# Decoder step: the first modulation matrix in four column items, inputs normalized by halves, query tiles in two halves

## The reference

```python
    mod = (jax.nn.silu(c) @ w_ada + b_ada)[:, None, :]
    sh1, sc1, gt1, sh2, sc2, gt2 = jnp.split(mod, 6, axis=-1)

    h = rmsnorm(x, g_mix) * (1 + sc1) + sh1
    qa, ka, va, fa, qb, kb, vb, rb, alr, ga, gb = split_cols(h @ w_in, IN_SIZES)
    ...
```

## Time and profile before

| | |
|---|---|
| time, median of 3 runs | 1292.62 us (1291.99 to 1293.03) |
| the profiled execution | 1289.96 us, of which the span of the profile is 1288.3 us |
| busy share of the span | PE 90%, VectorE 25%, ScalarE 14%, GpSimd 4% |
| bytes moved by DMA | 500.5 MB, 388 GB/s in the mean |

### The profile page before, as it was taken

The page is one execution under the profiler, slowest core; times in us unless marked ns, Lnnn a source line. Parts: engine busy times, 40 slices in busy tenths (PEclk is TensorE's granted clock), DMA queues, the critical chain, the costliest instruction groups (busy, mean ns, idle before and its releaser), DMA issues.

```text
span 1288.3 us, 15668 instructions
## 1 busy us (share of the span) xinstructions
PE 1153.6 (90%) x5948; PEld 567.6 (44%) x5948; DVE 324.2 (25%) x592; ACT 174.1 (14%) x344; POOL 48.2 (4%) x95
## 2 busy tenths in 40 slices
PE   5999999999999998889897979797988889797987
PEld 2788756687543442424242424333232424242433
DVE  2379965433122021011101110201111011101133
ACT  2132232100211100200020011002000200020102
POOL 1121122000000000000000000000000000000000
PEclk9999999999998999999999999999999999999998
DMA  9998999975979999999999999999999999999994
GB/s 349 352 375 284 378 330 394 398 317 192 411 318 416 412 418 416 420 415 421 414 423 414 422 414 421 415 419 417 418 419 416 419 415 422 414 421 411 417 417 180
DMA packets 109310, 500.52 MB, mean 388 GB/s; under 512 B 11721, under 2 KB 13879, under 8 KB 73808
## 3 DMA queue, kind: packets, MB, share of 16 engines
q1 hardware_dynamic: 102416, 478.39, 92.4%
q0 software_dynamic: 6576, 21.42, 4.6%
q10 hardware_dynamic: 272, 0.09, 0.0%
HBM read 496.48 MB, written 3.38 MB: 388 GB/s over the span
## 4 chain that ended last, share of the span: by engine, by line
PE 61%; DMA 21%; SPq 13%; issue 2%; ACT 2%; DVE 1%; DVEq 0%
PE ps L983 20%; DMA ring<-in_w_d 17%; SPq L2296 12%; PE ps L474 11%; PE ps L1043 8%; PE ps L1145 4%; PE ps L936 3%; PE ps L800 2%; PE ps L853 2%; DMA ring<-in_w_ada 2%; DMA ring<-in_w_gu 2%; PE ps L408 2%; PE ps L885 1%; PE ps L439 1%; PE ps L648 1%
## 5 line engine op out<-in xcount | busy, mean ns | idle before, releaser
L983 PE MATMUL ps<-ring,zone 128*64 128x512 f32 x2000 | 439.1, 594 | 22.4 <-DMA ring<-in_w_gu 22.4
L1043 PE MATMUL ps<-ring,oT 128*64 128x512 f32 x1024 | 232.7, 600 | 71.0 <-DMA ring<-in_w_d 70.3
L983 PEld LDWEIGHTS ps<-ring,zone 128*64 128x64 f32 x2000 | 139.8, 137 | 318.0 <-issue 277.5
L1043 PEld LDWEIGHTS ps<-ring,oT 128*64 128x64 f32 x1024 | 69.6, 137 | 231.8 <-issue 123.1
L1996 DVE TENSOR_SCALAR zone<-ps 128x1024 f32<-128x1024 f32 x15 | 18.4, 1225 | 587.2 <-PE ps L983 587.2
L474 PE MATMUL ps<-hT,ring 128*128 128x264 f32 x640 | 148.1, 389 | 2.1 <-DVE hT L1573 1.8
L474 PEld LDWEIGHTS ps<-hT,ring 128*128 128x128 f32 x640 | 119.8, 190 | 29.1 <-issue 7.7
L1412 ACT ACTIVATE attn<-zone 128x1024 f32<-128x1024 f32 x15 | 15.9, 1057 | 457.1 <-DVE zone L1996 457.1
L2013 DVE TENSOR_TENSOR zone<-zone,ps 128x264 f32<-128x264 f32 x56 | 24.1, 430 | 140.0 <-PE ps L1145 140.0
L408 PE MATMUL ps<-ident,zone 128*128 128x128 f32 (+3 forms) x212 | 32.3, 277 | 16.2 <-DMA zone<-in_b_alpha 10.6
L936 PE MATMUL ps<-zone,tok 128*128 128x224 f32 x224 | 44.2, 356 | 0.0
(11 more groups left out here) (389 smaller groups left out, 766.8 us busy)
## 6 DMA issues: line engine op xcount, KB each, us to landing
ring<-in_w_gu SPq DMA_DIRECT2D x250, 1024.0 KB, 19.8
ring<-in_w_d SPq DMA_DIRECT2D x124, 1024.0 KB, 18.4
ring<-in_w_ada SPq DMA_DIRECT2D x12, 2048.0 KB, 11.9
ring<-in_w_in SPq DMA_DIRECT2D x9, 2048.0 KB, 13.4
ring<-in_cache_k SPq DMA_DIRECT2D x32, 256.0 KB, 7.5
ring<-in_cache_k POOLq DMA_DIRECT2D x32, 256.0 KB, 6.5
ring<-in_cache_v SPq DMA_DIRECT2D x32, 256.0 KB, 9.7
ring<-in_cache_v POOLq DMA_DIRECT2D x32, 256.0 KB, 8.2
```

What stands on the lines that cost most here:

```text
L983: ins = pe.matmul(ps[64 * j:64 * j + CAP, c, :], xg[:, k, 2 * par + j, :], rows, start=False, stop=(k == KT - 1), skip_group_check=True)
L1043: ins = pe.matmul(ps[64 * j:64 * j + CAP, 4 + c, :], hidT[:, k, j * CAP:(j + 1) * CAP], w[:, j, k % 2, c * 512:(c + 1) * 512], start=(k == ...
```

## The change

1. **Items.** ada0 to ada3 now hold all 1024 rows and 512 columns each (pieces of 2 KB): ada0 the first 512 columns of the shift, ada1 the first 512 of the scale, ada2 and ada3 the second 512 of each. qa is loaded by halves of its rows (channel tiles 0 to 3, and 4 to 7) with all 512 columns; its first half comes after ada1, its second after ada3. The x tokens are loaded first of all.
2. **Modulation.** `modulate_first` makes 8 matmuls for each item, into one bank with four groups of 32 partitions that hold partial sums over the channel tiles k mod 4. ScalarE copies them to `mod0_rows`, and `sum_modulation` adds the four groups and turns them in one step: 8 matmuls for two items, with 128 columns of the rows as the stationary and 9 columns of `row_in_32` (1 where the partition mod 32 is the column) as the moving side.
3. **Halves.** After ada0 and ada1 the channel tiles 0 to 3 of `hT` are finished; after ada2 and ada3 the tiles 4 to 7. The query tiles q0 to q3 lie in four banks and are summed in two halves. PE's order is: q0, q1 (first halves), ada2, q2, ada3, q3, the second sum, then the four second halves.
4. **Start.** PE transposes cT ahead of the vectors, and VectorE makes `row_in_32` before anything from PE.

The diff (context lines left out):

```diff
@@ -63,7 +63,7 @@
-RING = ("ada0:0 ada1:1 ada2:2 ada3:3 qa:4 ka:5 K0:0 va:1 K1:2 fqk:3 K2:4 K3:0 vb:5 K4:2 rb:1 K5:4 K6:3 ga0:0 K7:5 "
+RING = ("ada0:0 ada1:1 qa:4 ada2:2 ada3:3 ka:5 K0:0 va:1 K1:2 fqk:3 K2:4 K3:0 vb:5 K4:2 rb:1 K5:4 K6:3 ga0:0 K7:5 "
@@ -174,6 +174,7 @@
+        mod0_rows = [part(zone, ALLP, 2112 + 512 * n, 512) for n in range(4)]
@@ -364,6 +365,8 @@
+        Q_BANKS = {"q0": 0, "q1": 1, "q2": 6, "q3": 7}
+        MOD0_BANKS = (5, 6, 5, 5)
@@ -410,15 +413,15 @@
-            pe.wait_ge(sig("vec_rows"), 16 * len(VEC_ROWS))
-            bank = vector_bank()
-            vector_filled(transpose(bank[:, 0:N_VEC], vec_rows), "vectors")
...
+            pe.wait_ge(sig("vec_rows"), 16 * len(VEC_ROWS))
+            bank = vector_bank()
+            vector_filled(transpose(bank[:, 0:N_VEC], vec_rows), "vectors")
@@ -452,16 +455,41 @@
+            def modulate_first(n):
+                item = f"ada{n}"
+                arrived(pe, item)
+                if n >= 2:
+                    pe.wait_ge(sig("mod0_rows"), 1 if n == 2 else 3)
+                w = slot_ap(item)[:, 0:4096].rearrange("p (k c) -> p k c", k=KT)
+                for k in range(KT):
+                    q = k % 4
+                    ins = pe.matmul(ps[32 * q:32 * q + 32, MOD0_BANKS[n], :], cT[:, k, :], w[:, k, :],
+                                    start=(k < 4), stop=(k >= 4), skip_group_check=True)
+                ins.then_inc(sig("mod0_full"), 1)
+                freed[item] = (sig("mod0_full"), n + 1)
+            def sum_modulation(half):
+                pe.wait_ge(sig("mod0_rows"), 2 * half + 2)
+                bank = vector_bank()
+                for n in range(2):
+                    for j in range(4):
+                        c0 = (4 * n + j) * 9
+                        ins = pe.matmul(bank[:, c0:c0 + 9], mod0_rows[2 * half + n][:, j * P:(j + 1) * P],
+                                        row_in_32[:, 0:9], start=True, stop=True)
+                vector_filled(ins, f"mod0_{half}")
...
-            modulate(0, ps[:, 5, :], range(2))
+            modulate_first(0)
...
-            modulate(0, ps[:, 5, :], range(2, 4))
-            turn_modulation(0)
+            modulate_first(1)
+            sum_modulation(0)
...
             def project(item, col, width, name, last=False, free=True):
@@ -469,8 +497,6 @@
-                    if name == "q0":
-                        pe.wait_ge(sig("h_even" if k % 2 == 0 else "h_odd"), k // 2 + 1)
@@ -482,10 +508,29 @@
+            def queries(i, half):
+                w = slot_ap("qa")[:, 0:512 * KT].rearrange("p (k c) -> p k c", k=KT)
+                for k in range(4 * half, 4 * half + 4):
+                    if i == 0:
+                        pe.wait_ge(sig("h_even" if k % 2 == 0 else "h_odd"), k // 2 + 1)
+                    ins = pe.matmul(ps[:, Q_BANKS[f"q{i}"], 0:T], w[:, k, i * P:(i + 1) * P], hT[:, k, :],
+                                    start=(k == 0), stop=(k == KT - 1), skip_group_check=True)
+                if half:
+                    scalar_filled(ins, f"q{i}")
...
-            tiles("qa", 0, "q", range(2))
+            queries(0, 0)
+            queries(1, 0)
+            modulate_first(2)
+            queries(2, 0)
+            modulate_first(3)
+            queries(3, 0)
+            sum_modulation(1)
...
-            tiles("qa", 0, "q", range(2, 4))
+            for i in range(4):
+                queries(i, 1)
+            freed["qa"] = (scalar_full, len(a_index))
@@ -1214,7 +1259,7 @@
-                return ps[:, (a_index[name] - 1) % 2, :]
+                return ps[:, Q_BANKS[name] if name in Q_BANKS else (a_index[name] - 1) % 2, :]
@@ -1245,15 +1290,18 @@
-                if n:
-                    act.wait_ge(vector_full, v_index["o_past1" if n == 1 else "modT1"])
+                act.wait_ge(vector_full, v_index["o_past1" if n == 1 else "modT1"])
...
-            take_rows(0, 5)
-            act.wait_ge(sig("gain1"), 1)
-            for k in range(1, KT, 2):
-                nc.scalar.activation(hT[:, k, 0:TP], hT[:, k, 0:TP], ACT.Identity, bias=modT[:, k, 0:1],
-                                     scale=gain1[:, k, 0:1]).then_inc(sig("h_odd"), 1)
+            for half in range(2):
+                for n in (2 * half, 2 * half + 1):
+                    act.wait_ge(sig("mod0_full"), n + 1)
+                    nc.scalar.activation(mod0_rows[n], ps[:, MOD0_BANKS[n], :], ACT.Copy)\
+                        .then_inc(sig("mod0_rows"), 1)
+                act.wait_ge(sig("gain1"), half + 1)
+                for k in (4 * half + 1, 4 * half + 3):
+                    nc.scalar.activation(hT[:, k, 0:TP], hT[:, k, 0:TP], ACT.Identity, bias=modT[:, k, 0:1],
+                                         scale=gain1[:, k, 0:1]).then_inc(sig("h_odd"), 1)
@@ -1537,8 +1585,10 @@
+            dve.wait_ge(sig("ident"), 1)
+            chain(V.tensor_reduce(row_in_32, ident[:, :].rearrange("p (q h) -> p h q", h=NE), AX_X, ALU.add))
+            give(V.tensor_copy(cT[:, :, 0:9], take("cT")[:, 0:9 * KT].rearrange("p (k c) -> p k c", c=9)), "cT")
...
-            give(V.tensor_copy(cT[:, :, 0:9], take("cT")[:, 0:9 * KT].rearrange("p (k c) -> p k c", c=9)), "cT")
@@ -1546,8 +1596,6 @@
-            dve.wait_ge(sig("ident"), 1)
-            V.tensor_reduce(row_in_32, ident[:, :].rearrange("p (q h) -> p h q", h=NE), AX_X, ALU.add)
@@ -1563,15 +1611,21 @@
-            modulation(0)
-            V.scalar_tensor_tensor(out=gain1[:, :, :], in0=modT[:, KT:2 * KT, :], scalar=1.0,
-                                   in1=across(vec["g_mix"], 9), op0=ALU.add, op1=ALU.mult).then_inc(sig("gain1"), 1)
-            dve.wait_ge(sig("gain1"), 1)
-            chain(V.tensor_tensor(hT[:, :, TP:T], hT[:, :, TP:T], gain1[:, :, 1:9], ALU.mult))
-            chain(V.tensor_tensor(hT[:, :, TP:T], hT[:, :, TP:T], modT[:, 0:KT, 1:9], ALU.add))
-            for k in range(0, KT, 2):
-                V.tensor_scalar(hT[:, k, 0:TP], hT[:, k, 0:TP], gain1[:, k, 0:1], modT[:, k, 0:1], ALU.mult,
-                                ALU.add).then_inc(sig("h_even"), 1)
+            for half in range(2):
+                tiles_ = slice(4 * half, 4 * half + 4)
+                bank = take(f"mod0_{half}")[:, 0:72].rearrange("p (n j c) -> p n j c", n=2, j=4)
+                give(V.tensor_tensor(modT[:, 0:2 * KT, :].rearrange("p (n k) c -> p n k c", n=2)[:, :, tiles_, :], bank,
+                                     vec["b_ada"][:, 0:2 * KT].rearrange("p (n k) -> p n k", n=2)[:, :, tiles_]
+                                     .unsqueeze(3).to_broadcast([P, 2, 4, 9]), ALU.add), f"mod0_{half}", then_read=True)
+                V.scalar_tensor_tensor(out=gain1[:, tiles_, :], in0=modT[:, KT + 4 * half:KT + 4 * half + 4, :], scalar=1.0,
+                                       in1=across(vec["g_mix"][:, tiles_], 9), op0=ALU.add, op1=ALU.mult)\
+                    .then_inc(sig("gain1"), 1)
+                dve.wait_ge(sig("gain1"), half + 1)
+                chain(V.tensor_tensor(hT[:, tiles_, TP:T], hT[:, tiles_, TP:T], gain1[:, tiles_, 1:9], ALU.mult))
+                chain(V.tensor_tensor(hT[:, tiles_, TP:T], hT[:, tiles_, TP:T], modT[:, tiles_, 1:9], ALU.add))
+                for k in (4 * half, 4 * half + 2):
+                    V.tensor_scalar(hT[:, k, 0:TP], hT[:, k, 0:TP], gain1[:, k, 0:1], modT[:, k, 0:1], ALU.mult,
+                                    ALU.add).then_inc(sig("h_even"), 1)
@@ -1721,7 +1775,7 @@
-            dve.wait_ge(sig("mod0_rows"), 1)
+            dve.wait_ge(sig("mod0_rows"), 4)
@@ -2176,6 +2230,11 @@
+            def load_queries(half, done):
+                rows = slice(4 * half, 4 * half + 4)
+                sp.dma_start(slot_ap("qa")[:, 0:512 * KT].rearrange("p (k c) -> p k c", k=KT)[:, rows, :],
+                             w_in[0].rearrange("(k p) c -> p k c", p=P)[:, rows, QA:QA + 512]).then_inc(done, 16)
@@ -2184,7 +2243,12 @@
-                if item[0:3] == "ada":
+                if item in ("ada0", "ada1", "ada2", "ada3"):
+                    c0 = (int(item[3:]) % 2) * D + (int(item[3:]) // 2) * 512
+                    sp.dma_start(dst[:, 0:4096].rearrange("p (k c) -> p k c", k=KT),
+                                 w_ada[0].rearrange("(k p) c -> p k c", p=P)[:, :, c0:c0 + 512])\
+                        .then_inc(landed[s], 16)
+                elif item[0:3] == "ada":
@@ -2192,10 +2256,7 @@
-                    for c, done in ((0, landed[s]), (256, sig("qa_second"))):
-                        sp.dma_start(dst[:, 0:512 * KT].rearrange("p (k c) -> p k c", k=KT)[:, :, c:c + 256],
-                                     w_in[0].rearrange("(k p) c -> p k c", p=P)[:, :, QA + c:QA + c + 256])\
-                            .then_inc(done, 16)
+                    load_queries(0, landed[s])
@@ -2222,13 +2283,12 @@
+            sp.dma_start(tok[:, 0:2, :], x_prompt[0].rearrange("(t p) d -> p t d", p=P)).then_inc(sig("x_tok"), 16)
```

(8 more changed lines are left out.)

## The result

The changed kernel takes 1294.56 us (median of 20 runs, 1293.07 to 1296.0), the kernel before in the same runs 1292.0 us (1289.88 to 1293.21). The ratio is 1.0022, 95% interval 1.0016 to 1.0028: slower, by some 2.5 us. I had forecast no change (1292.5 us). The time lies inside my range, even inside that of the forecast case, but the loss is just above the 0.2% up to which I called it no change, and its interval leaves no change out.

What follows compares the result with a forecast made beforehand. PE (busy 90%) and nearly full DMA were taken to compete, early PE time passing to the end about 1 to 1. Steps put k0 at 48.80 us against 48.87, -0.1, so median 1292.5 us; range 1290.0 to 1295.8.

Steps and rivals of the forecast that it cites:

- the forecast case: Whole kernel: k0 within -2 and +2 us of before, median 1290.6 to 1294.7 us, chance 0.67.
- start to x transposes, and these: PE's start: x transposes begin at 9.94 us, take 6.56 and end at 16.50.
- item 0: First 16 instructions on an ada item, PE still slow: 2.90 us, bounds 1.92 and 3.4.
- rstd matmuls: PE behind the first item: 0.95 us as before, ending at 20.35.
- first sum, to VectorE: 16 narrow instructions at 0.11 us each replace 4 transposes: 2.08 us to VectorE, where it was 0.76.
- first halves of q0, q1: PE behind the first sum: two half tiles of 8 instructions, 1.80 us each, 3.61 together.
- second halves: PE behind the second sum: four second halves of q0 to q3 in 7.22 us, ending at 48.80.
- rival (a): First-stage sums: 16 narrow instructions take 0.24 us and DMA leads; k0 2.0 to 3.8 us earlier; chance 0.14.
- The loads: Modulation items in 2 KB pieces at 386 GB/s: ada1 near 18 us, ada2 at 28.5, ada3 at 33.9.
- (b): q2/q3 in the first stage: PE waits for ada3 landing after 34.09 us; median 1295.2 to 1297; chance 0.19.
- The exchange rate: First stage to kernel end: a microsecond of PE before 360 us moves the end about 1 to 1.
- Rival (c): First stage gains as claimed, but VectorE's key stage or DMA absorbs it; 0.1 us at stake, no separate chance.

Runs made afterwards that it cites:

- e10: The kernel before with 8 useless 9-column matmuls (16 instructions) ahead of its turn of the modulation rows, the kernel of e5 run again; 1295.61 us, ratio 1.0043.
- e6: The kernel before with 2 useless 512-column matmuls (4 instructions) ahead of its turn of the modulation rows; 1294.15 us, ratio 1.0019.
- e9: The changed kernel with useless 256-column matmuls ahead of and behind the first sum, and q3's first half moved behind the second sum; 1292.52 us, ratio 1.0008.
- e4: The changed kernel with warming matmuls before the first transpose, a filled first VectorE gap, and q3's first half moved behind the second sum; 1293.94 us, ratio 1.0016.
- e11: The changed kernel with the start order of the kernel before (ada0 ahead of x, vectors ahead of cT); 1297.86 us, ratio 1.0051.
- after_again: The changed kernel run once more, unchanged, for a second profile; 1295.16 us in one run.
- e3: The changed kernel's items and loads, but no q work between them: four items, both sums, then whole q tiles; 1299.42 us, ratio 1.0068.
- e1: The changed kernel with 3 useless 128x512 matmuls in each of the two waits for VectorE's gain; 1292.86 us, ratio 1.0008.
- e8: The kernel before with useless 256-column matmuls in its three first-stage waits (ada3, copy of the rows, VectorE's gain); 1292.0 us, ratio 1.0005.
- e7: The kernel before with only the change's start: x loaded first, cT ahead of the vectors, row_in_32 made first; 1295.15 us, ratio 1.0029.
- e2: The changed kernel with 22 useless 128x128 matmuls ahead of the first transpose, while PE waits for SiLU; 1293.43 us, ratio 1.0020.
- e5: The kernel before with 8 useless 9-column matmuls (16 instructions) ahead of its turn of the modulation rows; 1295.21 us, ratio 1.0027.

## Why the prediction was wrong

My forecast had k0 at 48.80 us; it came at 53.13, 4.33 later. By its own steps, each from one start to the next:

| step | predicted us | measured us | difference |
|---|---|---|---|
| start to x transposes, and these | to 16.50 | to 16.46 | -0.04 |
| item 0 | 2.90 | 3.57 | +0.67 |
| rstd matmuls | 0.95 | 1.62 | +0.67 |
| item 1, copy of its rows | 2.64 | 2.64 | 0 |
| first sum, to VectorE | 2.08 | 2.06 | -0.02 |
| VectorE to q | 1.69 | 1.52 | -0.17 |
| first halves of q0, q1 | 3.61 | 5.41 | +1.80 |
| item 2, q2, item 3, q3 | 7.44 | 7.57 | +0.13 |
| second sum, VectorE | 3.77 | 3.40 | -0.37 |
| second halves | 7.22 | 8.88 | +1.66 |

**Where it failed.** The step is "q0 and q1: 3.61" and "four second halves 7.22". I took 0.2255 us for every q instruction from a row at full clock and never asked whether PE's clock would survive the new gaps; none of the terms of my range stood for it. Twice it didn't: 5.41 and 8.88 us, 3.46 us more than I had summed. That the 9-column matmuls between the two waits bring the clock down, and not the waits alone, is shown by e10 against e6. In after's own order the first drop goes when wide matmuls stand on both sides of the sum (e9). The second is less certain in its coming (e4 and e11 had none), and what decides it wasn't isolated. It is a cost of the new sums that isn't in their rows: the first sum took 2.06 us to VectorE and the second 1.89, where I had 2.08 for each, and they brought nearly as much again behind them.

The Trainium skill ("TensorE: Matmul & The Clock Gate", the section on the HAM clock gate) says that the clock is halved when PE idles and is full again once it works. After's and e10's rows agree on the levels. The page speaks of idling, and e10 against e6 adds that PE busy with 16 narrow instructions didn't hold the clock as 4 wide ones did (19.45 against 18.04 us behind them).

**The slow start.** The second miss is a mis-sized term: item 0 and the rstd matmuls, 5.19 us instead of 3.85. I let the slow phase cost what it cost in the kernel before, as if one execution's figure were fixed. It isn't. With the same code up to there these two steps took 5.19 us in after, 4.95 in after_again, 4.61 in e3, 4.29 in e9 and 3.67 in e1, and the first two items with the old start 4.82 in the kernel before, 4.96 in e10, 5.38 in e6 and 6.04 in e8. My 3.85 lies inside this scatter, towards its low end, and the profile of after at its high end. Whether coming to item 0 earlier makes it slower, too, can't be told from so few profiles (item 0 took 3.00 us with the old start in e11). My bound of 3.4 for item 0 was short of 3.57, and rstd had no bound.

**What held.** The transposes began at 9.95 (9.94 predicted), with no wait for the vectors (9.77). The reason that I gave, shorter pieces in front of them, has two pairs of profiles: with the new start PE waited for the vectors until 10.73 us behind 8 KB pieces (e7) and not at all behind 2 KB ones (after), and with the old start they were there at 10.62 (before) and 8.89 (e11). The narrow matmuls cost 0.12 us each, as the 128-wide rows said, not 0.015; so rival (a) fell at its condition. The loads: 34.61 us for ada3 against 33.9, and 28.09 for ada2 against 28.5. That the sum for ada3 came so near is partly luck: e7 shows that loading x first moves the last item by 1.5 us with 8 KB pieces, and I had costed that at nothing. ada1, which I had near 18, came only at 19.76 in e4. The landing of ada3 is the side of (b), 0.5 us later than I wanted it, but PE was itself late and never waited (item 3 at 37.11 with no wait). So (b) named the right sign by the wrong mechanism; its mark, a wait of PE for `in_w_ada`, is absent.

By the rule that I quoted from the Trainium skill ("DMA: Bandwidth & Descriptors", Specifications) ada3 would have landed at 32.1, as an estimate. e3's 34.61 is 2.5 us later, but 1.5 of this may be the order of the loads (e7), so no run here isolates what the shorter pieces cost.

**The exchange rate.** One to one held, to about a microsecond, where no drop of the clock came later. In after the marker is 4.38 late, the loads 4.38, and 1.55 more come from a drop of the clock that after_again didn't have. Rival (c) has nothing for it. In e1 the marker is 3.0 late and the span 2.9; in e2 2.5 and 2.7; in e10 3.8 and 3.9; in e8 and e9 the span takes 0.5 and 1.2 more than the marker.

**Why no version beat the kernel before.** ada3's landing sets a floor for k0: 34.61, 1.92 for the item, 0.72 and 1.95 for copy and sum, 1.80 for q3's half, which covers VectorE, and 7.2 for the second halves make 48.2, 0.7 us better than 48.87. The best stage tried (e4) had 49.48. The gain of an early start is thus limited by the loads and the sum even with a perfect clock, and e1, e8 and e9 are the same as before within their intervals.

**Open.** The stage of after is 4.4 us late against the one profile of before, but its median only 2.5. Before's median in the three sets of runs (1291.79, 1291.41, 1291.08) lies 1.1 to 1.8 above its profiled execution, while e1's profiled one lies on its own median. The mean clocks say that here, too, it is the clock: before's profiled execution had 0.995, and of the 73 runs of before the 32 with 0.995 took 1290.6 us in the mean, the 21 with 0.993 took 1292.5. So typical executions of before lose something to the clock that the profiled one didn't. Where they lose it no profile shows; e8 speaks against the three waits that it filled. The drop at 325 to 340 us was in the profiles of after, e3, e4, e5, e6 and e11, and not in before, after_again, e1, e2, e7, e8, e9 and e10. What decides it wasn't tried.

## What to carry to other kernels

When an edit puts small matmuls between two waits of TensorE, cost not only these but the wide ones that follow: here 3.5 us, more than either sum. Useless matmuls in the gaps took as long as they saved (e1). Work that is needed anyway costs nothing there, but doesn't hold the clock for certain: e4's moved half tile ran without a drop, e9's with one. So check in the profile that the granted clock holds behind each gap, and in more than one execution, since the first profile here overstated the loss. And before pulling an early stage forward, find when its last load lands; that, and not the engine's start, is the floor.

## What the runs showed of the hardware

- Behind 16 instructions with 9 columns (1.95 us) between waits of 0.72 and 1.6 to 1.8 us TensorE fell from 2.4 to 1.2 GHz in the profiles of after, after_again, e2, e10 and e11; behind 4 instructions with 512 columns (1.98 us) in the same place it did not (e6). The instructions behind took 1.4 to 1.8 us more in the first four, 3.0 in e11. With no wait ahead of them, or none behind, it fell in some profiles and not in others.
- Behind waits for a load of 3.3 to 4.4 us the next item of 16 instructions took 2.8 to 3.5 us instead of 1.92 (e3, e5, e7); behind waits of 2.13 and 2.28 us it took 1.92 (before, e10), but 3.19 behind one of 2.19 us that had 16 instructions with 9 columns ahead of it (e3).
- TensorE starts slow: 24 transposes took 6.58 us cold and 4.19 after warming matmuls (e4), while the granted clock read 1.00 in the cold case.
- With the x tokens loaded first and 8 KB pieces behind them, the last item landed 1.5 us later (e7) than with the tokens second. Why was not tried. Small loads beside 2 KB pieces were there at 8.89 us (e11), beside 8 KB ones in the same order at 10.62 (before).
